# Twenty blocks of the modulation weighed by VectorE under the projections of layer 0, the gates and convolutions moved under its input projection, and the constants in one load

## What is computed

```python
c_act = silu(c)                                        # c: (1, 1024)
for layer in range(2):
    mod = c_act @ ada_w[layer] + ada_b[layer]          # 1024 x 6144, six rows of 1024
    sh1, sc1, g1, sh2, sc2, g2 = split(mod, 6)
    h = rms_norm(x, norm_mix_g[layer]) * (1 + sc1) + sh1
    y = mlstm_moba_mixer(h, ...)                       # layer 1: diff_attention_mixer
    x = x + g1 * y
    h = rms_norm(x, norm_ffn_g[layer]) * (1 + sc2) + sh2
    x = x + g2 * peer_ffn(h, ...)                      # 8 heads, 16 of 16384 experts a token

# mlstm_moba_mixer: z = h @ w_in; q, k of the mLSTM through a causal convolution of 4 taps
# and silu; two gate columns a head; mLSTM of 4 heads; attention of 8 heads; y @ w_out
```

## Time and profile before

| | us |
|---|---|
| median of 3 runs | 2736.96 |
| lowest, highest | 2731.71, 2740.73 |
| profiled execution | 2728.6 |
| its span, first to last instruction | 2726.8 |

### The profile page before, as it was taken

The page is one execution under the profiler, slowest core; times in us unless marked ns, Lnnn a source line. Parts: engine busy times, 40 slices in busy tenths (PEclk is TensorE's granted clock), DMA queues, the critical chain, the costliest instruction groups (busy, mean ns, idle before and its releaser), DMA issues.

```text
span 2726.8 us, 24920 instructions
## 1 busy us (share of the span) xinstructions
PE 2222.6 (82%) x8378; PEld 1092.3 (40%) x8378; DVE 1218.7 (45%) x3018; ACT 850.5 (31%) x2249; POOL 612.3 (22%) x586
## 2 busy tenths in 40 slices
PE   5977799987779988979988977777799976666665
PEld 1742147432325545536455422222574643222221
DVE  1023014676756696664777677764203421011100
ACT  1022211444434574444654434343102310000000
POOL 1000000444343343332343444443100100000000
PEclk8987899999999999999999999999899897777888
DMA  9432852899999999999999999999542037999998
GB/s 356 141 120 93 338 220 97 326 421 421 421 421 390 421 399 413 420 415 421 417 373 408 404 421 422 421 421 423 191 155 93 1 123 301 428 429 428 429 428 344
DMA packets 111348, 907.57 MB, mean 333 GB/s; under 512 B 17762, under 2 KB 18048, under 8 KB 20928
## 3 DMA queue, kind: packets, MB, share of 16 engines
q0 software_dynamic: 77072, 550.75, 49.6%
q1 hardware_dynamic: 34160, 355.38, 31.9%
HBM read 904.98 MB, written 6.06 MB: 334 GB/s over the span
## 4 chain that ended last, share of the span: by engine, by line
PE 46%; DMA 34%; DVE 10%; ACT 6%; issue 2%; POOL 1%; SPq 0%; DVEq 0%; ACTq 0%; POOLq 0%
DMA arena<-in_peer_uv_dram,arena 19%; DMA arena<-in_moe_pieces_dram 14%; PE summed L993 13%; PE gp L807 7%; PE gp L797 5%; PE gp L1057 4%; DVE y L1993 4%; PE gp L1053 2%; PE gp L783 2%; PE gp L1275 2%; PE turned L894 1%; PE summed L906 1%; PE scores L873 1%; ACT arena L1509 1%; PE gp L793 1%
## 5 line engine op out<-in xcount | busy, mean ns | idle before, releaser
L993 PE MATMUL summed<-arena 128*128 128x512 f32 x2048 | 994.8, 619 | 219.6 <-ACT arena L1509 196.8
L1993 DVE CUSTOM_DVE_ANT_0 y<-arena,h 128x1024 f32<-128x1024 f32 x512 | 627.2, 1225 | 384.4 <-DMA arena<-in_peer_uv_dram,arena 346.8
L746 POOL DMA_INDIRECT arena<-in_peer_uv_dram,arena x512 | 570.1, 1114 | 905.4 <-PE summed L993 810.6
L993 PEld LDWEIGHTS summed<-arena 128*128 128x128 f32 x2048 | 365.1, 193 | 774.5 <-ACT arena L1509 436.2
L1503 ACT ACTIVATE arena<-arena 128x1 f32<-128x1 f32 x512 | 102.6, 200 | 513.2 <-DVE arena L1993 512.4
L1275 PE MATMUL gp<-arena,mod 128*32 128x512 f32 x1024 | 166.9, 788 | 114.6 <-DMA arena<-in_moe_pieces_dram 113.4
L1509 ACT ACTIVATE arena<-cst,arena 128x128 f32<-128x128 f32 x512 | 205.5, 401 | 16.8
L807 PE MATMUL gp<-hT,arena 128*128 128x256 f32 x896 | 200.2, 386 | 3.2 <-ACT hT L1392 2.1
L807 PEld LDWEIGHTS gp<-hT,arena 128*128 128x128 f32 x896 | 173.4, 194 | 29.3 <-ACT hT L1392 3.1
L2275 DVE TENSOR_TENSOR mod<-mod,gp 128x512 f32<-128x512 f32 x8 | 5.5, 688 | 385.0 <-ACT mod L1690 385.0
L1506 ACT ACTIVATE arena<-arena 128x1 f32<-128x1 f32 x512 | 150.7, 294 | 16.6
(11 more groups left out here) (367 smaller groups left out, 2132.0 us busy)
## 6 DMA issues: line engine op xcount, KB each, us to landing
arena<-in_moe_pieces_dram SPq DMA_DIRECT2D x96, 2048.0 KB, 25.6
arena<-in_w_slots_dram SPq DMA_DIRECT2D x48, 2048.0 KB, 9.0
mod<-in_w_parts_dram SPq DMA_DIRECT2D x24, 1024.0 KB, 9.0
arena<-in_w_parts_dram SPq DMA_DIRECT2D x24, 1024.0 KB, 9.3
arena<-in_peer_uv_dram,arena POOLq DMA_INDIRECT x512, 14.2
t_rep<-t_rows POOLq DMA_DIRECT2D x1, 3066.0 KB, 11.6
arena<-t_rep POOLq DMA_DIRECT2D x1, 2304.0 KB, 13.1
na_rep<-na_rows POOLq DMA_DIRECT2D x1, 1778.0 KB, 12.0
```

The lines of the kernel that those rows point to most:

```text
L746: pool.indirect_dma_start(rowbuf[b], None, a["peer_uv"].rearrange("l n d -> (l n) d"), bass.IndirectOffsetOnAxis(ap=idx[:, col(n):col(n) + ...
L993: mm = pe.matmul(op[:, b, :], diag[:, n % DIAGS, :], rowbuf[n % ROWS][:, D + b * 512:D + (b + 1) * 512], start=n % SLOTS == 0, stop=n % SL ...
L1993: v.tensor_tensor_reduce(y[:, t, :], rowbuf[n % ROWS][:, 0:D], h[:, t, :], 1.0, 0.0, ALU.mult, ALU.add, dots[:, c:c + 1]).then_inc(udot, 1)
```

## The change

The four `ada` blocks stay as they are. The other twenty (`vec`) are done by VectorE in `weigh(i)`: for each output column it sums, over the eight rows that a partition holds, weight times `cact`, in one tensor_scalar and seven scalar_tensor_tensor over 128x512, with one more for the bias over 24x512. TensorE then adds the 128 partitions in one matmul with ones. A `vec` slot's place in the ring is free when VectorE has weighed it (`acc_done`), and `slot_free` chooses between the two semaphores. Fourteen are loaded and weighed during `in0`, two ahead of each of its slots in the stream; their matmuls come two behind each. Three go with `out0` and three with `wq0`. The gates' matmuls move ahead of `in0`, their chain and the convolutions under its first slots. The T5 matmuls and adds move behind the first norm, and the writes of both bias tables wait for h. Ten small constants are packed in `cst` by the host, and three loads stand ahead of the weights. The eight row buffers are used in another order.

```diff
+ROW_HOMES = (2, 3, 6, 7, 4, 5, 0, 1)
...
+    for n in range(4):
+        slots.append(("ada", view("ada_w", 0, n * CH), [("part", n), ("quarters", n)]))
+    vecs = [("vec", view("ada_w", l, n * CH), [("sum" if l == 0 or n >= 10 else "row", l, n)])
+            for l in range(2) for n in range(12) if l or n >= 4]
...
-    ada(0, 0, 4)
+    def vec(n):
+        for _ in range(n):
+            slots.append(vecs.pop(0))
     w = ("ev_w_in", 0)
+    vec(2)
     cols("in0", w, 0, 0)
+    vec(2)
     cols("in0", w, 512, 4)
+    vec(2)
     rows("in0", w, 1024, ("zn", 0))
...
+    vec(2)
     rows("in0", w, 3080, ("zn", 1024))
-    ada(0, 4, 12)
-    ada(1, 0, 12)
-    for n in range(2):
-        rows("out0", ("ev_w_out", 0), n * CH, ("y", n * CH))
+    rows("out0", ("ev_w_out", 0), 0, ("y", 0))
+    vec(1)
+    rows("out0", ("ev_w_out", 0), CH, ("y", CH))
+    vec(2)
     for n in range(4):
         cols("wq0", ("peer_wq", 0), n * CH, 4 * n)
+        if n < 3:
+            vec(1)
...
-        rowbuf = [arena[:, 2048 * b:2048 * (b + 1)] for b in (2, 3, 4, 5, 6, 7, 0, 1)]
+        rowbuf = [arena[:, 2048 * b:2048 * (b + 1)] for b in ROW_HOMES]
...
+        vec_slots = phase_slots["vec"]
+        in_order = list(phase_slots["ada"])
+        for m, n in enumerate(phase_slots["in0"]):
+            in_order += [n] + vec_slots[2 * m:2 * m + 2]
+        in_order += phase_slots["out0"] + vec_slots[14:17] + phase_slots["wq0"] + vec_slots[17:20]
+        in_order += phase_slots["mem"] + phase_slots["in2"] + phase_slots["out2"]
...
+        def slot_free(engine, n):
+            if n in vec_slots:
+                engine.wait_ge(acc_done, vec_slots.index(n) + 1)
+            else:
+                engine.wait_ge(gemm_done, group_end(n))
...
+        weighed_w = [flat_h[:, CH * (i % 4):CH * (i % 4 + 1)] if i < 17 else flat_y[:, CH * (i - 17):CH * (i - 16)] for i in range(VECS)]
...
+            sync.dma_start(cst[:], a["cst"]).then_inc(loaded, 16)
+            sync.dma_start(ada_b[:], a["ada_b"].rearrange("l (n c) -> (l n) c", n=12)).then_inc(loaded, 16)
             sync.dma_start(x[:], a["x"][0].rearrange("(t p) n -> p t n", p=P)).then_inc(loaded, 16)
-            sync.dma_start(cst[:], a["cst"]).then_inc(loaded, 16)
-            sync.dma_start(cact[:], a["c"][0].rearrange("(k p) -> p k", p=P)).then_inc(loaded, 16)
-            sync.dma_start(gains[:], a["gains"]).then_inc(loaded, 16)
...
-            sync.dma_start(gw36[:, :, 4:36], a["w_r2_2"][0].rearrange("(k p) n -> p k n", p=P)).then_inc(loaded, 16)
...
-                    sync.wait_ge(gemm_done, group_of[n - RING] + len(slots[n - RING][2]))
-                if n == phase_slots["ada1"][0]:
-                    sync.wait_ge(gemm_done, last_group["ada0"])
-                    sync.dma_start(ada_b[:], a["ada_b"][1].rearrange("(n c) -> n c", n=12)).then_inc(loaded, 16)
+                    slot_free(sync, n - RING)
...
-            pool.dma_start(na_rows, na_pad).then_inc(na_w, 16)
-            pool.wait_ge(na_w, 16)
+            pool.wait_ge(h_ready, T)
+            pool.dma_start(na_rows, na_pad).then_inc(bias_w, 16)
+            pool.wait_ge(bias_w, 16)
-            pool.dma_start(na_rep, bass.AP(tensor=na_rows.tensor, offset=0, ap=[[0, GRID_W], [1, W]])).then_inc(na_w, 16)
+            pool.dma_start(na_rep, bass.AP(tensor=na_rows.tensor, offset=0, ap=[[0, GRID_W], [1, W]])).then_inc(bias_w, 16)
             pool.wait_ge(t5_sum, 1)
-            pool.dma_start(t5_rows.rearrange("(g h) n -> h g n", g=3), t5_out.rearrange("p (g n) -> p g n", g=3)).then_inc(t5_w, 16)
-            pool.wait_ge(t5_w, 16)
-            pool.dma_start(t5_rep, bass.AP(tensor=t5_rows.tensor, offset=0, ap=[[0, P], [1, 12 * TW]])).then_inc(t5_w, 16)
-            pool.wait_ge(t5_w, 32)
-            pool.wait_ge(na_w, 32)
+            pool.dma_start(t5_rows.rearrange("(g h) n -> h g n", g=3), t5_mask.rearrange("p (g n) -> p g n", g=3)).then_inc(bias_w, 16)
+            pool.wait_ge(bias_w, 48)
+            pool.dma_start(t5_rep, bass.AP(tensor=t5_rows.tensor, offset=0, ap=[[0, P], [1, 12 * TW]])).then_inc(bias_w, 16)
+            pool.wait_ge(bias_w, 64)
...
-                    pool.wait_ge(gemm_done, group_of[phase_slots["wq0"][b // 2]] + 2)
+                    r = ROW_HOMES[b] // 2
+                    slot_free(pool, max(k for k in range(phase_slots["mem"][0]) if k % RING == r))
...
+                        elif grp[0] == "quarters":
                             pe.wait_ge(gemm_moved, g)
                             m = grp[1]
+                            pe.matmul(bank, quarter.to_broadcast([P, P]), ada_part[m % 2], start=True, stop=False)
+                            mm = pe.matmul(bank, ident[0:24, m:m + 1].to_broadcast([24, P]), ada_b[:, :], start=False, stop=True)
+                        elif grp[0] in ("sum", "row"):
+                            i = vec_slots.index(n)
+                            r = 32 * (grp[2] % 4)
+                            pe.wait_ge(acc_done, i + 1)
                             if grp[0] == "sum":
-                                dst, one, bias = bank, quarter.to_broadcast([P, P]), ident[0:12, m:m + 1].to_broadcast([12, P])
+                                mm = pe.matmul(bank, ones1[:, 0:1].to_broadcast([P, P]), weighed_w[i], start=True, stop=True)
                             else:
-                                r = 32 * (m % 4)
-                                dst, one, bias = bank[r:r + 1, :], quarter, ident[0:12, m:m + 1]
-                            pe.matmul(dst, one, ada_part[m % 2], start=True, stop=False)
-                            mm = pe.matmul(dst, bias, ada_b[:, :], start=False, stop=True)
+                                mm = pe.matmul(bank[r:r + 1, :], ones1[:, 0:1], weighed_w[i], start=True, stop=True)
...
             project("ada")
-            pe.wait_ge(t5_in, 16 * (NA_HEADS + 3))
-            for g in range(DIL_GROUPS):
-                mm = pe.matmul((sp_ if g < 2 else op)[0:DIL_HPG, g % 2, 0:TW], t5_tab[:, g * DIL_HPG:(g + 1) * DIL_HPG], t5_hot,
-                               start=True, stop=True)
-            mm.then_inc(t5_mm, 1)
             keep_clock("ada", 6)
             turn_h(0)
             hT_ready()
-            pe.wait_ge(t5_sum, 1)
-            project("in0")
+            pe.wait_ge(t5_in, 16 * (NA_HEADS + 3))
+            for g in range(DIL_GROUPS):
+                mm = pe.matmul((tp if g < 2 else op)[0:DIL_HPG, g % 2, 0:TW], t5_tab[:, g * DIL_HPG:(g + 1) * DIL_HPG], t5_hot,
+                               start=True, stop=True)
+            mm.then_inc(t5_mm, 1)
+            gates()
+            for m in range(7):
+                project("in0", slice(m, m + 1))
+                if m == 0:
+                    gate_columns()
+                project("vec", slice(2 * m, 2 * m + 2))
...
             project("out0")
+            project("vec", slice(14, 17))
+            pe.wait_ge(gemm_moved, group_end(vec_slots[16]))
-            keep_clock("out0", 15)
+            keep_clock("out0", 12)
...
+            project("vec", slice(17, 20))
...
@@ ScalarE @@
+            gates_in()
+            for m in range(7):
+                move("in0", slice(m, m + 1))
+                if m == 0:
+                    gates_rest()
+                if m in (1, 2):
+                    for c in range(4 * m - 4, 4 * m):
+                        silu(c)
+                move("vec", slice(2 * m, 2 * m + 2))
...
+            def weigh(i):
+                n = vec_slots[i]
+                _, l, m = slots[n][2][0]
+                w = ring[:, n % RING, :].rearrange("p (k c) -> p k c", k=KT)
+                acc = weighed_w[i]
+                if 4 <= i < 17:
+                    v.wait_ge(gemm_done, group_end(vec_slots[i - 4]))
+                v.wait_ge(w_landed[n % RING], 16 * (n // RING + 1))
+                link(v.tensor_scalar(acc, w[:, 0, :], cact[:, 0:1], None, ALU.mult))
+                link(v.scalar_tensor_tensor(out=acc[0:24, :], in0=ada_b[:, :], scalar=ident[0:24, 12 * l + m:12 * l + m + 1],
+                                            in1=acc[0:24, :], op0=ALU.mult, op1=ALU.add))
+                for k in range(1, KT):
+                    ins = v.scalar_tensor_tensor(out=acc, in0=w[:, k, :], scalar=cact[:, k:k + 1], in1=acc, op0=ALU.mult, op1=ALU.add)
+                    if k < KT - 1:
+                        link(ins)
+                ins.then_inc(acc_done, 1)
...
+            def weigh_and_gate():
...
+                weigh(0)
                 v.wait_ge(gates_f, 1)
...
+                weigh(1)
                 v.wait_ge(gates_l, 1)
...
+                weigh(2)
+                v.wait_ge(gemm_moved, group_end(phase_slots["in0"][0]))
+                for c in range(4):
                     convolve(c)
+                weigh(3)
+                weigh(4)
+                v.wait_ge(gemm_moved, group_end(phase_slots["in0"][1]))
+                for c in range(4, 8):
+                    convolve(c)
+                for i in range(5, 14):
```

(12 more changed lines are left out.)

179 lines of the change are left out of this document (85 added, 94 removed).

## The result

| | before | changed kernel |
|---|---|---|
| median of the runs, us | 2734.34 (2731.46 to 2740.73) | 2636.21 (2629.22 to 2642.73) |
| ratio, 95% interval | | 0.9638 (0.9605 to 0.967) |
| profiled execution: its time / span, us | 2728.6 / 2726.8 | 2642.7 / 2640.8 |
| first row product on TensorE, us | 490.74 | 400.94 |

The change saves 98 us on the medians, where 86 was forecast. The profiled execution of the changed kernel is the slowest of its four. A second profile of the same kernel, taken later, has a span of 2634.9.

A forecast was written before the change was run, and what follows sets the result against it. The memory-bound retrieval (1400 us at 414 GB/s) bounds the kernel; shortened earlier stages bring its first row from 490.74 to 404.8, saving 85.9 us: 2642.7 from the profiled 2728.6, 2651 on the median; range 2628 to 2675.

The forecast's parts named there:

- Start: Before the projection: first weights at 14.5 us, norm at 39.9, projection from 66.3 against 66.0 before.
- Price of a block: VectorE's time to weigh one modulation block: 6.4 us, bounded by 5.8 and 7.2.
- Projection: Layer 0's projection stage: TensorE's 111.9 us plus waits and slow clock, ending at 195.5 us, bounds 179 to 205.
- forecast wait of 8.5 at the second slot: Projection: second slot loads only after weighed block 1, beside bias replicas; lands at 91.5, TensorE ready at 83.
- forecast wait of 5 behind the convolutions: Projection: fourth slot waits for block 5, behind both convolution groups; lands at 128 against 123.
- rival B: Projection bound by loads and slots, 6.5 us per load, ending at 207 or 212; 2662 to 2668 us; chance 0.13.
- mLSTM and head norms: Projection's end to attention: mLSTM 24.7 us, then 19.8 us to the attention, starting at 240 against 260.4.
- Attention: Layer 0's attention without blocks between heads: 38 us, nearly all at half clock, bounds 27 and 45.
- The row of 0.52: Profile row of the second attention: TensorE busy 21.16 of 21.2 us at granted clock 0.52; basis for half-level attention.
- Rival A: Clock at full level through mLSTM and attention: 11 and 4 us less, 2636 us; chance 0.20.
- Output projection: After attention: 28.5 us plus 3 for a slow start; residual starts at 310, 90.4 us earlier than before.
- First rows: First retrieval rows, behind blocks 17 to 19 and a later top-k: 4.5 us uncovered delay (3 to 12).

The follow-up runs named there:

- the gates' run: Changed kernel with the gates' Exp, Ln and second Exp ahead of ScalarE's copy of the first projection slot: 2629.08 us, ratio 0.963.
- five edits: Changed kernel with gates' Exp/Ln earlier, bias copies behind attention, blocks 17 to 19 before last wq0 slot, softmax exponentials earlier, convolutions later: 2608.22 us, ratio 0.9551.

## Why the prediction was right, and where it was not

The direction, the mechanism and the range held: the time lay 15 us under the forecast and 8 above the low end. No sign of being wrong came: a block costs 6.68 us, under 7.5; TensorE waits for VectorE twice in the projection, not in most slots; from the first row to the end it is 2239.9 us for 2236. By its own steps:

**Start.** The first weights came at 17.3 us, not at 14.5 (bounds 13 to 18). The term of bytes was too small: between the weights' issue at 2.1 us and 17.3 the DMA engines moved 5.6 MB at 369 GB/s, where I had counted 4.5 MB at 414. The blocks took 20.8 us instead of 24.7, since only the first ran at the half level. The norm at 38.95 against 39.9 is right by these two errors together. The transposes took 3.77 us as before. T5 took 5.2 us for 4.1, all at the half level, and the gates' matmuls took 9.84 and 8.39 for 7.07 (0.71 granted in the first profile), so the projection began at 69.1 and 68.1, not at 66.3.

**Price of a block.** 6.4 forecast, 6.68 measured. The bounds hold.

**Projection.** 195.5 forecast, 208.8 and 204.4 measured: outside the bound of 205 in the first profile and inside it in the second. This is the step that came out too short. I followed the loads and VectorE by hand, but not ScalarE's program. The forecast wait of 8.5 at the second slot was right in kind, as the gates' run shows, and hidden under the missed one of 7.6. The forecast wait of 5 behind the convolutions came one slot earlier and was 6.75, with 3.1 more at the fourth slot and 3.6 at the seventh, where I had VectorE ahead. (The sum takes 13.8 us for two waits told as 8.5 and 5, which make 13.5.) The sum of VectorE's work, 108 us, is close: 109.2 from 59.3 us on, which has 2 us of the T5 adds in it. Of rival B, the cause was partly there (slots handed on late), but not loads of 6.5 us: with five edits the same 21 loads fit into 119.6 us.

The Trainium skill, page "DMA: Bandwidth & Descriptors", section "Anatomy of one DMA", gives the fit of about 2.0 us plus bytes over 436 GB/s for transfers issued by GpSimd. Applied to these, which SyncE issues, it would have landed a 2 MB load in an estimated 6.8 us. The third slot's took 8.07 from the end of block 3, nearer to the row of 9.0; the measurement decides.

**mLSTM and head norms.** 44.5 us forecast, 42.7 and 42.9 measured. In the first profile the mLSTM has 23.8 of these for 24.7, the way to the attention 18.9 for 19.8.

**Attention.** 38 forecast, 26.1 and 21.4 measured, below the lower bound of 27. Two terms failed: the level, taken from one row of the second attention, and the entry, for which I took 8.5 us to the first turned piece where it took 4.2. The row of 0.52 was true and did not carry over: that stretch stays at the half level for 21 us, this one for 9, for less, or not at all. What decides between these stays open. The rule of the Trainium skill that I had set against it, on page "TensorE: Matmul & The Clock Gate", section "Part 1: The HAM clock gate", that activity releases the throttle, agrees with this trace: TensorE was busy for all of 257.0 to 266.3 and the full level followed. Rival A was right about the attention, nearly in the first profile and wholly in the second, and wrong about the mLSTM, which ran mostly at the half level as forecast (0.68 granted from its start to the attention). Its 2636 us are the measured median, but not by its own account: it had the projection end at 195.5.

**Output projection.** The residual started at 306.5, not 310: no slow start came (27.70 us, all at the full level), so it came 28.8 us behind the start of the output projection, for 32. Block 16 waited 8.5 us for its load and was summed 1.1 us after the projection's last matmul.

**First rows.** 4.5 us forecast; measured 5.0 by the distance from wq0's start to the first row, 73.9 for 68.9. The covered part was as told: block 19 waited 15.5 us for its load, and VectorE then still had 12.8 us of idle time.

**The sum.** In the first profile the projection ended 13.3 us too late for the forecast. From there the mLSTM and head norms took 1.8 us less than forecast, the attention 11.9 and the output projection 3.2, and the rest 0.3: the first row at 400.94 against 404.8. The profiled time, 2642.7, is the forecast sum to a tenth, but only because the retrieval and what follows were 3.8 us longer than before, which the 3.9 us of the earlier first row make good. The direction and the way in which the time is saved were right; the close agreement is luck, of errors that cancel. On the medians the kernel did 12 us better, since its profiled execution was its slowest and the one before was 6 us under its own median; the second profile of the changed kernel (2636.85) is near the median.

## What to carry to other kernels

When work is moved under another stage, follow every engine's program there, also that of the engine that only copies: a wait of 10 us came from a 0.6 us copy placed ahead of a 0.4 us Exp. Two waits that end at the same point hide one another, so an edit that removes one can measure as nothing until the other goes too; test them together before dropping either. And with a ring of buffers, check that each engine consumes in the order of loading: the same fourteen blocks on TensorE cost some 50 us more or less by that alone (2724.80 and 2672.08 us).

## What the runs showed of the hardware that I had not expected

The same program has its TensorE at different levels in different executions of one stage: the attention took 26.1 us (granted clock 0.80) and 21.4 us (1.00) in two profiles of one kernel, and the first row moved by 8.5 us. In the run with more products ahead the level fell in this stage although TensorE had been busy for 15.45 us of 16.3 at the full level and for 3.15 of the 4.6 us that followed, so the products ahead did not hold it. The 2 MB load of the second slot took 14.2 us with the end of a bias copy and four small loads beside it, and at most 8.1 without. A scalar_tensor_tensor on 24 rows takes as long (0.74 us) as on 128 (0.75), and the sixteen matmuls of a modulation block on TensorE take 1.92 us at the full level and 3.54 to 3.64 at the half one, which gives the level away in this kernel's timelines.
